# Gate and up pieces walked by contraction block, and the first weights behind each mixture converted in halves

## The reference, cut to what matters

```python
h = rms_norm(x, norm1_g[1]) * (1 + sc1) + sh1        # "n_odd"
q, k, v = split(h @ w_in, 3)                         # "odd_in", width 3072, behind moe0
...
x = x + g2 * grouped_moe(h, ...)                     # "moe0", "moe1": 16 experts of width 512, 2 for a token
...
def swiglu_ffn(x, norm_g, w_in, w_out):              # "pre0", "post0", "pre1", "post1", width 2816
    gate, up = split(rms_norm_2(x, norm_g) @ w_in, 2)
    return (silu(gate) * up) @ w_out
...
proj = u @ a_w_in                                    # "a_in", width 2816, behind pre0
```

## Time and profile before

| What | Value |
|---|---|
| Median of 3 runs | 2104.72 us (2102.3 to 2104.86) |
| The profiled execution | 2100.68 us, its span 2098.9 us |
| PE busy | 1952.4 us, 93% |
| DVE, ACT busy | 1175.7 us (56%), 941.9 us (45%) |
| DMA | 476.43 MB, mean 227 GB/s |
| Mean granted PE clock | 0.973 |

### The profile page before, as it was taken

How to read it: one execution, slowest core, us unless ns; L and a number is a source line. 1 busy time by engine, 2 the same in 40 slices (tenths; PEclk the granted TensorE clock), 3 DMA queues, 4 the chain that set the end, 5 groups by cost and what they waited for, 6 DMA issues and landing times.

```text
span 2098.9 us, 32837 instructions
## 1 busy us (share of the span) xinstructions
PE 1952.4 (93%) x13922; PEld 1425.8 (68%) x13922; DVE 1175.7 (56%) x1616; ACT 941.9 (45%) x1338; POOL 75.7 (4%) x129
## 2 busy tenths in 40 slices
PE   6998988888998988889999999899999999999999
PEld 4777525223977332238888977778887888878887
DVE  5767632344877323446556464666555676537555
ACT  4344444345363443454445453354445444445442
POOL 2040000000010000000000000000000000200000
PEclk9999998999999989999999999999999999999999
DMA  9977899997958799995555500165554555505552
GB/s 347 341 252 270 308 386 341 386 372 275 336 160 297 278 383 388 372 324 191 182 194 171 155 1 4 32 210 183 183 193 155 201 187 193 167 1 180 183 198 102
DMA packets 261346, 476.43 MB, mean 227 GB/s; under 512 B 8512, under 2 KB 118144, under 8 KB 255824
## 3 DMA queue, kind: packets, MB, share of 16 engines
q1 hardware_dynamic: 251264, 431.81, 58.8%
q0 software_dynamic: 9936, 42.51, 6.0%
HBM read 472.15 MB, written 2.14 MB: 226 GB/s over the span
## 4 chain that ended last, share of the span: by engine, by line
PE 75%; DMA 12%; DVE 6%; ACT 4%; issue 2%; SPq 0%; POOL 0%; DVEq 0%; ACTq 0%; POOLq 0%
PE psum L1113 16%; PE psum L1515 8%; PE psum L1115 8%; DMA experts<-in_exp_w_down 5%; PE psum L1130 4%; PE psum L1132 4%; PE psum L1131 4%; PE psum L1079 3%; PE psum L1081 3%; PE psum L1080 3%; DMA experts<-in_exp_w_up 3%; DMA experts<-in_exp_w_gate 3%; PE psum L1068 2%; PE psum L1070 2%; PE psum L1069 2%
## 5 line engine op out<-in xcount | busy, mean ns | idle before, releaser
L2823 DVE TENSOR_TENSOR w_lo<-ring,w_hi 128x2048 fp32r<-128x2048 f32 x193 | 440.7, 2289 | 189.5 <-ACT w_hi L2142 188.1
L1113 PE MATMUL psum<-h_both,w_hi 128*128 128x512 f32 x1408 | 499.8, 399 | 1.6 <-DVE h_both L3515 1.3
L2142 ACT ACTIVATE w_hi<-ring 128x2048 fp32r<-128x2048 f32 x193 | 368.7, 1914 | 216.4 <-PE psum L1132 119.8
L1115 PE MATMUL psum<-h_both,w_lo 128*128 128x256 f32 x1408 | 395.3, 281 | 0.0
L1113 PEld LDWEIGHTS psum<-h_both,w_hi 128*128 128x128 f32 x1408 | 264.5, 188 | 68.4 <-issue 1.7
L2336 ACT ACTIVATE pool<-experts 128x512 f32 x336 | 186.2, 621 | 230.3 <-PE psum L1515 86.1
L3227 DVE COPY pool<-experts 128x512 f32 x384 | 142.6, 423 | 255.0 <-PE psum L1515 113.3
L1115 PEld LDWEIGHTS psum<-h_both,w_lo 128*128 128x128 f32 x1408 | 265.9, 189 | 1.4
L2164 ACT ACTIVATE pool<-psum 128x512 f32<-128x512 f32 x88 | 52.6, 598 | 261.5 <-PE psum L1115 261.5
L1079 PE MATMUL psum<-w_hi,h_both 128*128 128x512 f32 (+1 forms) x352 | 142.6, 405 | 9.3 <-DVE w_lo L2823 5.2
L1515 PE MATMUL psum<-experts,pool 128*32 128x512 f32 x1024 | 124.2, 611 | 19.6 <-DMA experts<-in_exp_w_down 17.7
(11 more groups left out here) (452 smaller groups left out, 2864.9 us busy)
## 6 DMA issues: line engine op xcount, KB each, us to landing
experts<-in_exp_w_gate SPq DMA_DIRECT2D x64, 1024.0 KB, 13.4
experts<-in_exp_w_up SPq DMA_DIRECT2D x64, 1024.0 KB, 14.3
experts<-in_exp_w_down SPq DMA_DIRECT2D x64, 1024.0 KB, 15.1
ring<-in_ffn_pre_w_in SPq DMA_DIRECT2D x44, 1024.0 KB, 5.1
ring<-in_ffn_post_w_in SPq DMA_DIRECT2D x44, 1024.0 KB, 5.1
ring<-in_ada_w SPq DMA_DIRECT2D x24, 1024.0 KB, 6.9
ring<-in_ffn_pre_w_out SPq DMA_DIRECT2D x22, 1024.0 KB, 4.8
ring<-in_ffn_post_w_out SPq DMA_DIRECT2D x22, 1024.0 KB, 4.9
```

The costliest lines, as they stand in the source:

```text
L1113: pe.matmul(o.rearrange("p (s n) -> p s n", s=2), wh[:, k, fs], h_both[:, :, k, :], start=k == 0, stop=False, skip_group_check=True)
L1115: m = pe.matmul(o[:, 0:T], wl[:, k, fs], h_hi[:, k, :], start=False, stop=k == KD - 1, skip_group_check=True)
L2142: act.activation(w_hi[:, (s["split"] + r) % 3, :], piece(s["pieces"][r]), ACT.Copy)\
L2823: dve.tensor_tensor(w_lo[:, slot, :], piece(s["pieces"][r]), w_hi[:, slot, :].bitcast(F32), ALU.subtract).then_inc(sem("w_lo"), 1)
```

## The change

In `gate_up` the loop over k is outside and f inside, in every gate and up piece. For each k there are four matmuls: both parts for f = 0, both parts for f = 1, then `w_lo` for f = 0 and for f = 1. Only at k = 0 of a stage's first piece does `w_lo` for f = 0 come second, followed, in pre0, post0 and post1, by a wait for the block of the norm that frees bank 5. The first piece of odd_in and of a_in has k outside and f inside as well; their other pieces stay.

Behind moe0 and moe1 the first piece is converted in two halves of 1024 columns on ACT and DVE. DVE makes both `var` parts and the first half in pass 23 ahead of `added(1)`, with the wait for `m_act` ahead of the half, and the second half between the first tile's diagonal and the second tile's reciprocal. The semaphores `rw_low` and `rw_sig` become one, `rw_inputs`, with the same order of signals; those lines are left out here.

```diff
-                        if kind in ("feat", "shift"):
+                        if kind in ("feat", "shift") and n == 1:
+                            for k in range(ks):
+                                pe.wait_ge(sem("h_split_lo"), SPLIT_BASE[split] + k + 1)
+                                for f in range(2):
+                                    fs, dst = slice(P * f, P * f + P), bank(pair + lo // 256)[:, T * f:T * f + T]
+                                    pe.matmul(dst, wh[:, k, fs], h_hi[:, k, :], start=k == 0 and f == 0, stop=False, skip_group_check=True)
+                                    pe.matmul(dst, wh[:, k, fs], h_lo[:, k, :], start=False, stop=False, skip_group_check=True)
+                                    m = pe.matmul(dst, wl[:, k, fs], h_hi[:, k, :], start=False, stop=k == ks - 1, skip_group_check=True)
+                        elif kind in ("feat", "shift"):
...
-                    for f in range(2):
-                        o, fs = bank(4 + 2 * j + f), slice(P * f, P * f + P)
-                        for k in range(KD):
-                            if n == 0 and f == 0:
-                                pe.wait_ge(sem("h_split_lo"), SPLIT_BASE["n_" + nm] + k + 1)
...
+                    for k in range(KD):
+                        if n == 0:
+                            pe.wait_ge(sem("h_split_lo"), SPLIT_BASE["n_" + nm] + k + 1)
+                        both_parts(0, k)
+                        if n == 0 and k == 0:
+                            low_weights(0, k)
+                            if "n_" + nm in NORM_EIGHT:
+                                pe.wait_ge(sem("h_split_lo"), SPLIT_BASE["n_" + nm] + NORM_EIGHT["n_" + nm].index(5) + 1)
+                        both_parts(1, k)
+                        if n > 0 or k > 0:
+                            low_weights(0, k)
+                        m = low_weights(1, k)
                     m.then_inc(sem("w_used"), 1)
...
+            def split_in_halves(nm):
...
+                for half, done_ in ((0, "w_half"), (1, "w_split_hi")):
+                    cols = slice(PIECE // 2 * half, PIECE // 2 * half + PIECE // 2)
+                    act.activation(w_hi[:, slot, cols], piece(s["pieces"][0])[:, cols], ACT.Copy).then_inc(sem(done_), 1)
...
-            split_piece("odd_in", 0, 0)
+            split_in_halves("odd_in")
...
                     dve.tensor_scalar(norm_diag[:, t, :], ident, rstd[:, t:t + 1], None, ALU.mult).then_inc(sem("norm_xn"), 1)
+                    if t == 0 and behind_first:
+                        behind_first()
...
+            def half_split(nm, half):
+
+                s = STAGES[nm]
+                slot, cols = s["split"] % 3, slice(PIECE // 2 * half, PIECE // 2 * half + PIECE // 2)
+                if half == 0:
+                    dve.wait_ge(sem("w_half"), AFTER_MOE.index("n_" + {"odd_in": "odd"}.get(nm, nm)) + 1)
+                else:
+                    dve.wait_ge(sem("w_split_hi"), s["split"] + 1)
+                m = dve.tensor_tensor(w_lo[:, slot, cols], piece(s["pieces"][0])[:, cols], w_hi[:, slot, cols].bitcast(F32), ALU.subtract)
...
+                    if p == 23:
+                        for t in range(NT):
+                            first_part(then_norm, t)
+                        dve.wait_ge(sem("m_act"), len(ACT_TILES) * (done + MOE_PASSES))
+                        half_split(then, 0)
                     if p in (19, 23):
                         added(p // 4 - 4)
-                dve.wait_ge(sem("m_act"), len(ACT_TILES) * (done + MOE_PASSES))
-                split_piece(then, 0, 0)
...
-            norm("n_odd")
+            norm("n_odd", lambda: half_split("odd_in", 1))
```

More of the change, by code:

```diff
@@ L1647, in _ @@
             par = rwkv_par
-            pe.wait_ge(sem("rw_low"), 2)
+            pe.wait_ge(sem("rw_inputs"), 2)
             for i in range(6):
@@ L2438, in _ @@
             moe("moe1", "n_moe1", "n_pre0")
-            split_piece("pre0", 0, 0)
+            split_in_halves("pre0")
             split_piece("pre0", 1, 1)
@@ L2591, in step, with first_part, diag_of @@
                 dve.wait_ge(sem("dve_step"), done[0])
-            def diag_of(nm, tiles=range(NT)):
-                n = NORMS.index(nm)
-                def first_part(t):
-                    mine = [i for i, q in enumerate(SQ[nm]) if q[0] == t]
-                    if len(mine) == 2:
-                        dve.wait_ge(sem("norm_ss"), SQ_BASE[nm] + mine[0] + 1)
-                        dve.tensor_scalar(var[:, t:t + 1], ss[:, 2 * t:2 * t + 1], 1.0 / D, EPS, ALU.mult, ALU.add)\
-                           .then_inc(sem("norm_var"), 1)
+            def first_part(nm, t):
+                mine = [i for i, q in enumerate(SQ[nm]) if q[0] == t]
+                if len(mine) == 2:
+                    dve.wait_ge(sem("norm_ss"), SQ_BASE[nm] + mine[0] + 1)
+                    dve.tensor_scalar(var[:, t:t + 1], ss[:, 2 * t:2 * t + 1], 1.0 / D, EPS, ALU.mult, ALU.add)\
+                       .then_inc(sem("norm_var"), 1)
+            def diag_of(nm, tiles=range(NT), behind_first=None):
+                n = NORMS.index(nm)
                 together = (nm, 0) in VAR_AT
                 for t in tiles:
-                    if t == 0 or not together:
-                        first_part(t)
-                    if t == 0 and together:
-                        first_part(1)
+                    if nm not in AFTER_MOE:
+                        if t == 0 or not together:
+                            first_part(nm, t)
+                        if t == 0 and together:
+                            first_part(nm, 1)
                     if SQ[nm]:
@@ L2637, in norm @@
                 else:
-                    diag_of(nm, (1,) if nm in FIRST_TILE.values() else range(NT))
+                    diag_of(nm, (1,) if nm in FIRST_TILE.values() else range(NT), behind_first)
                 if nm in WHOLE:
@@ L3174, in router, with moe @@
                 ordered()
-            def moe(nm, norm_nm, then):
+            def moe(nm, norm_nm, then, then_norm):
                 layer = int(nm[-1])
@@ L3349, in _ @@
             router(1)
-            moe("moe1", "n_moe1", "pre0")
-            norm("n_pre0")
+            moe("moe1", "n_moe1", "pre0", "n_pre0")
+            norm("n_pre0", lambda: half_split("pre0", 1))
             swiglu("pre0", "a_in")
```

45 lines of the change are left out of this document (26 added, 19 removed).

## The result

The changed kernel took **2089.63 us** (median of 4 runs, 2087.2 to 2090.55) against 2104.77 for the kernel before beside it (4 runs, 2102.3 to 2104.86): a ratio of 0.9933, 95% interval 0.9919 to 0.9947. Its profiled execution took 2087.2, span 2085.4.

The account below looks back on a forecast made before the run. PE was taken as full inside the swiglu pieces but idle ahead of both norms. Terms 1.38 + 1.36 + 1.14 + 0.75 = 4.6 us off the 2104.72 median gave 2100.1, own range 2098 to 2102.5, 8-in-10 range 2095.0 to 2104.3.

Parts of the forecast that it names:

- All other gate and up pieces: In the four swiglu stages, 704 groups of four reordered matmuls: taken as 0, with ends of -9 and +9 us.
- if it is the change of width: Condition on a gate and up pair's unexplained 0.006 us: half of it goes, -0.006 per four matmuls, at most -0.013.
- The pair's 0.006 us: In gate and up pieces, unexplained part of a pair's 0.3532 us; it may belong to h's two separate runs, which stay.
- Rival 1: Reordered gate and up matmuls run faster: at half the excess 4.6 us more gain, 2095.5 us; chance 0.14.
- The edges: Gains at the norms behind moe0 and moe1 and at first pieces: 1.38 + 1.36 + 1.14 + 0.75 = 4.6 us.
- halves, moe1 and moe0: Behind both mixtures, converting the first piece in halves starts the norm 1.38 us (moe1) and 1.36 us (moe0) earlier.
- room ahead of the sums: Behind moe1, DVE's first half is ready 0.5 us before PE lets the sums begin.
- second odd piece behind the first: In odd_in, the second piece starts 6.57 us after the first instead of 7.71, limited by its low part: 1.14 us gained.
- first piece of pre0, post0, post1: First gate pieces of these stages lose their excess over mid-stage pace, 0.2 us each.
- Rival 2: The start is hidden: the half meets DVE late or something else holds PE behind the warming matmuls; 2102.8 us; chance 0.21.
- Rival 3: Reordered matmuls cost more in all four swiglu stages, by exchange of banks and weights; up to 2109.3 us; chance 0.09.
- Rival 4: PE's clock falls because banks are cycled; with a tenth of gate and up work slowed, 2150 us; chance 0.01.

Follow-up runs that it names:

- one run of 512: 512-column matmuls read one run of h_hi instead of two, against the changed kernel: old order in all but a stage's first piece 2097.03 us, new order 2092.06 us.
- twos: The changed kernel's order, two 512-column then two 256-column matmuls, against the kernel before: 2089.63 us, ratio 0.9933.
- The edges' kernel: Changed kernel with all gate and up pieces but a stage's first back in the old order 512, 256, 512, 256: 2095.28 us, 0.9968 against the kernel before.
- the two runs with up pieces in pairs: Changed kernel with up pieces, but for a stage's first, in the old order 512, 256, 512, 256: 2084.72 us; with 12 instead of 20 warming matmuls too: 2084.23 us.
- fours: Changed kernel with four 512-column matmuls, then four of 256, for two contraction blocks at a time: 2091.31 us, ratio 0.996.
- 320 columns: Changed kernel with the low-weight matmuls 320 columns wide instead of 256: 2135.96 us in the old order, 2130.32 us in the new.
- a single quad: The edges' kernel with two 512-column then two 256-column matmuls at the head of each gate piece, alternating widths behind: 2096.03 us.
- the best version: Changed kernel with up pieces, but for a stage's first, in the old order and 12 instead of 20 warming matmuls behind both mixtures: 2084.23 us, 0.9925 against the kernel before.
- sixteens: Changed kernel with all sixteen 512-column matmuls of a piece ahead of all sixteen 256-column ones: 2079.51 us; with 12 warming matmuls 2087.42 us.
- shifted pairs: The edges' kernel with each gate piece's first half shifted by one: a 512-column matmul ahead, one more 256-column matmul at that half's end: 2094.42 us.

## Why the prediction was wrong

**The failed step** is "All other gate and up pieces", which ends in "I take 0". It measured 6.46 us in the gate and up pieces (9.6 ns a quad in the middle of the stages) and 1.99 in the down pieces behind them (53 ns each in the middle): 8.45 us, where the sum of 4.6 us has nothing. The measured gain came near the lower end of that step's bounds, -9 us, and the condition written beside it, "if it is the change of width", pointed the right way: the order of the widths does it, though not at a fixed price for each change. Three things went wrong in weighing it:

- The two neighbours that bracketed the quads (the gather and the odd projection) have matmuls of one width each. Neither could say anything about alternating widths, which was what the pair had and they had not. They settled the question of the bank, rightly, and it was taken for the other.
- The pair's 0.006 us was given to the two runs of h. The run with one run of 512 shows exactly the old length. (The rows cited for the 0.227 give 3.42 / 15 = 0.228 and so leave 0.005; the trace's nanoseconds give 353.3 - 227 - 120 = 6.3.)
- Rival 1 was priced at half of the excess of 13 ns per quad. In effect 12 of the 13 went: 8.45 us over 704 quads. Three quarters of that is in gate and up. The rest comes because the down piece, all of 512 columns, started slow behind pairs (241, 237, 233, 236 ns in its first four) and is at 227 from its third matmul on behind twos; the forecast had no term for it. Rival 1 at its full end would have been 2104.7 - 4.6 - 9 = 2091; the measured 2089.6 is within the spread of this kernel's runs of that.

**The edges were right** in nearly every term:

| term | forecast | trace |
|---|---|---|
| halves, moe1 and moe0 | 1.38, 1.36 | 1.36, 1.34 |
| a half on DVE, on ACT | 1.20, 1.03 | 1.23, 1.00 |
| room ahead of the sums | 0.5 | 0.51 |
| second odd piece behind the first | 6.57 | 6.57 |
| first piece of pre0, post0, post1 | 0.2 each | 0.20, 0.20, 0.20 |
| of a_in, pre1 | 0.17, 0 | 0.09, 0 |

The first odd piece in 5.8 and the wait of 0.8 behind it came as 5.83 and 0.74, by starts. The excesses named for the other first pieces add up to 0.77, where the prediction wrote 0.75; they gave 0.69. The 0.2 of three of them is partly luck: of the excess over a piece of the same kernel's middle 0.085 stayed in pre0 (5.658 against 5.573), and 0.077 came from the order of the widths, which the forecast had at nothing. The forecast left out 0.11 at each norm: with the wait gone the norm's row takes 3.73 instead of 3.84. The edges' kernel gained 6.7 us by its ratio, interval 4.2 to 9.3, where the terms say 4.6 and its trace 4.7, with 1.0 more from three fast pieces in each of pre0, post0 and post1.

**Rival 2** (the start is hidden) fell: nothing idle ahead of line 1032, and the sums still waited 0.51 us for PE. **Rival 3** (slower quads) fell with the quads. **Rival 4** fell: the granted clock is 1.00 in both stretches of swiglu work while the banks change at each matmul. The Trainium skill, TensorE: Matmul & The Clock Gate, section A second HAM failure mode: psum-queue depth-cycling, tells of a clock that goes up and down in a kernel that cycles through banks, and puts it down to short idle times of PE between groups of matmuls. The two stretches have neither: PE was busy for 127.00 of 127 us and 130.00 of 130.

**What stays open** is the mechanism behind the two rhythms. Shown is that widths in turn are needed for the loss, that the bank, the reuse of an operand and the shape of the moving operand have no part in it, and that the same pairs run at 346.6 or 353.3 ns by what ran ahead of them: behind twos, in the two runs with up pieces in pairs, all 79 that were entered from a last spacing of 112 or 113 were fast, and all seven entered from 119 or 120 slow. That is a sign by which to tell them, not a cause. A fixed price for each change of width fails on fours and on the fast pairs, and a bound by the load of the weights fails on 320 columns. What in the engine holds a rhythm, why some first pieces in twos end on the one kind of quad and some on the other, why a single quad leads into the slow rhythm (nothing between one and eight was tried), and why fours stay slow is open.

## What to carry to other kernels

Where PE is full, price a new order of matmuls by the spacing of starts, and test whether each row used as a bound holds the one thing that changes: a few ns per matmul, times 2816 here, and what they did to the pieces behind, outweighed every wait that the change removed. Before an order is called slow, look for places in the trace where the same order runs faster, since what ran ahead of it may set its pace. Check that in every stage, not only in the middle of one: the best version's gain was a third of what the middle chunks promised. And when a bound's condition is written down ("if it is the change of width"), put the rival at its full end, not at half.

## What the runs showed of the hardware

- Alternating 512 and 256 columns takes 353.3 or 346.6 ns a pair, and keeps the one or the other for whole pieces. Behind twos it was the fast one where the last matmul had taken 112 or 113 ns and the slow one where it had taken 119 or 120. Rows of one width take 227 and 120. The Trainium skill, TensorE: Matmul & The Clock Gate, section Back-to-back issue gap, gives columns / 2.4 + 2.5 ns for an isolated matmul, by which (an estimate) the two would take 216 + 109 = 325 in any order; it also says that with weight loads both instructions set the spacing. The rows, in which each matmul has its own load, show more than 325 ns in every order, and a dependence on what ran before.
- The order reaches into the next piece. A down piece that was not edited took 5450 ns behind twos or fast pairs, 5486 behind fours and 5467 behind sixteens. Behind slow pairs it took 5503 in the middle of the stages, but 5467 where the pairs ended on 236 113 instead of 232 118 (pre0's first down piece of the kernel before, and the runs with one quad or shifted pairs), and 5449 in post0's first.
- A moving operand in two separate runs of 256 costs nothing against one run of 512, and a change of bank at each matmul costs nothing.
- Half of a 128x2048 conversion cost 1.23 of 2.29 us on DVE and 1.00 of 1.90 on ACT: halving it adds 0.1 to 0.2 us in all.
